# Layer 0 and 1 routing over 112 candidate sums, and more of the gathered rows' dots during routing than with the lots

## The reference

```
def peer(h, w_q, sub_keys, u_tab, v_tab):
    t = h.reshape(b * n, d)
    q = (t @ w_q).reshape(b * n, PEER_HEADS, 2, PEER_KEY_DIM)        # 8 heads
    s = jnp.einsum('thcd,hcnd->thcn', q, sub_keys)                   # 2 x 128 scores a head
    sv, si = lax.top_k(s, PEER_TOPK)                                 # 16 of each
    cand = (sv[:, :, 0, :, None] + sv[:, :, 1, None, :]).reshape(b * n, PEER_HEADS, 16 * 16)
    score, pos = lax.top_k(cand, PEER_TOPK)
    i1 = jnp.take_along_axis(si[:, :, 0], pos // PEER_TOPK, axis=-1)
    i2 = jnp.take_along_axis(si[:, :, 1], pos % PEER_TOPK, axis=-1)
    expert = i1 * PEER_KEYS + i2
    gate = softmax(score)
    ...
        act = gelu(einsum('td,thkd->thk', tb, jnp.take(u_tab, eb, axis=0)))
        return einsum('thk,thkd->td', gb * act, jnp.take(v_tab, eb, axis=0))
```

## Time and profile before

| | us |
|---|---|
| median of 3 runs | 3322.03 |
| lowest, highest run | 3318.63, 3327.59 |
| profiled execution | 3330.15 |
| its span | 3328.3 |
| TensorE busy in the span | 3179.4 |
| VectorE busy | 2511.7 |
| ScalarE busy | 1465.8 |
| GpSimd busy | 1061.4 |

### The profile page before, as it was taken

How to read it: one execution, slowest core, us unless ns; L and a number is a source line. 1 busy time by engine, 2 the same in 40 slices (tenths; PEclk the granted TensorE clock), 3 DMA queues, 4 the chain that set the end, 5 groups by cost and what they waited for, 6 DMA issues and landing times.

```text
span 3328.3 us, 52861 instructions
## 1 busy us (share of the span) xinstructions
PE 3179.4 (96%) x20142; PEld 2921.5 (88%) x20142; DVE 2511.7 (75%) x4061; ACT 1465.8 (44%) x1864; POOL 1061.4 (32%) x706
## 2 busy tenths in 40 slices
PE   7999889999999999999999999999988999999999
PEld 5998689856777899999999999997868898989998
DVE  6877568686764489988749999897665797757777
ACT  5434344322443333366643333334234567864443
POOL 0110000010000278877673334451000698721110
PEclk9999899999999999999999999999999999999999
DMA  8984157461012267799999999994203578999996
GB/s 320 332 307 170 51 190 247 157 227 64 1 39 102 98 233 272 264 326 383 363 399 390 381 378 411 410 410 169 89 1 121 182 242 294 388 367 335 352 342 232
DMA packets 305610, 835.27 MB, mean 251 GB/s; under 512 B 22432, under 2 KB 185504, under 8 KB 254368
## 3 DMA queue, kind: packets, MB, share of 16 engines
q1 hardware_dynamic: 180096, 534.82, 44.2%
q0 software_dynamic: 67968, 247.49, 19.3%
q10 hardware_dynamic: 57376, 50.72, 4.5%
HBM read 750.10 MB, written 82.84 MB: 250 GB/s over the span
## 4 chain that ended last, share of the span: by engine, by line
PE 73%; DVE 13%; DMA 5%; ACT 3%; issue 2%; POOL 2%; SPq 1%; ACTq 0%; DVEq 0%; POOLq 0%
PE ps L3369 16%; PE ps L862 7%; PE ps L3352 6%; PE ps L1688 5%; PE ps L2909 5%; PE ps L873 4%; PE ps L2310 3%; PE ps L2933 3%; PE ps L3354 3%; PE ps L319 3%; DMA gates<-arena 3%; PE ps L2911 3%; PE ps L1430 2%; PE ps L1412 2%; DVE arena L2968 2%
## 5 line engine op out<-in xcount | busy, mean ns | idle before, releaser
L2883 POOL TENSOR_TENSOR arena_split<-ring,arena_split 128x1024 fp32r<-128x1024 f32 x228 | 569.5, 2512 | 886.5 <-ACT arena_split L2801 883.7
L2933 PE MATMUL ps<-xT_split,arena_split 128*128 128x384 f32 x2048 | 535.1, 337 | 4.0 <-ACT xT L2831 3.2
L3369 PE MATMUL ps<-arena_split 128*128 128x384 f32 x3072 | 532.7, 334 | 1.0 <-DVE arena_split L3292 1.0
L3369 PEld LDWEIGHTS ps<-arena_split 128*128 128x128 f32 x3072 | 532.4, 188 | 1.3 <-issue 1.3
L286 DVE TENSOR_TENSOR arena_split<-ring,arena_split 128x2048 fp32r<-128x2048 f32 x128 | 292.9, 2291 | 245.8 <-ACT arena_split L280 244.9
L3263 ACT ACTIVATE arena_split<-ring 128x2048 fp32r<-128x2048 f32 x126 | 241.7, 1918 | 504.3 <-PE ps L3369 314.7
L280 ACT ACTIVATE arena_split<-ring 128x2048 fp32r<-128x2048 f32 x128 | 244.4, 1915 | 378.3 <-PE ps L862 133.3
L2933 PEld LDWEIGHTS ps<-xT_split,arena_split 128*128 128x128 f32 x2048 | 372.1, 188 | 5.3 <-issue 4.2
L3289 DVE TENSOR_TENSOR arena_split<-ring,arena_split 128x2048 fp32r<-128x2048 f32 x128 | 293.3, 2291 | 98.9 <-ACT arena_split L3263 92.8
L557 POOL DMA_DIRECT2D arena<-in_side_weights x152 | 82.8, 546 | 824.2 <-DVE arena L577 288.5
L2909 PE MATMUL ps<-hT_split,arena_split 128*128 128x448 f32 x1024 | 338.7, 379 | 6.7 <-POOL arena_split L2883 4.5
(11 more groups left out here) (353 smaller groups left out, 6377.1 us busy)
## 6 DMA issues: line engine op xcount, KB each, us to landing
ring<-in_weights SPq DMA_DIRECT2D x396, 1024.0 KB
arena<-in_side_weights POOLq DMA_DIRECT2D x152, 512.0 KB
gates<-arena SPq DMA_DIRECT2D x76, 512.0 KB
arena<-gates SPq DMA_DIRECT2D x32, 768.0 KB
arena<-activations SPq DMA_DIRECT2D x64, 384.0 KB
activations<-xT ACTq DMA_DIRECT2D x128, 112.0 KB
arena<-gates SPq DMA_DIRECT2D x32, 448.0 KB
arena<-activations SPq DMA_DIRECT2D x64, 224.0 KB
```

Source lines behind the costliest of these rows:

```text
L2883: pool.tensor_tensor(low, self.raw(f)[:, j, :], high.bitcast(F32), ALU.subtract)\
L2933: mm = pe.matmul(k.ps[:, j, 0:self.T], self.u[:, 2 * (f % 2) + j, a, t * P:(t + 1) * P], self.h[b][:, t, :], start=n == 0, stop=n == 3 * D ...
L3369: mm = pe.matmul(k.ps[:, t, self.from_token:self.from_token + self.T], self.v[:, f % 2, a, j * D + t * P:j * D + (t + 1) * P], self.weight ...
```

## The change

There are two parts.

The sums are formed only where they can be among the 16 largest, in two blocks: list places 0 to 3 of the first list with all 16 of the second (64 sums), and places 4 to 15 of the first with 0 to 3 of the second (48 sums). That makes 112 in place of 256, and `top` runs over rows of 112. A place found below 64 splits as before (by 16); one from 64 on splits by 4, and its first part is place / 4 - 12. This applies to both layers.

The dots of layer 0 are spread anew: 20 in place of 12 in each of tiles 1 to 3, so at each pause one or two, and one dot with each lot. That is 60, 48 and 20 in place of 36, 72 and 20. `pair_of` follows, and with it the places of the gathers in GpSimd's queue.

```diff
+PAUSES = 14
+BLOCKS = ((0, 4, 16, 0), (4, 16, 4, 64))
+CANDIDATES = 112
...
-        self.per_tile, self.pauses = 12, 0
+        self.per_tile, self.pauses = 20, 0
...
-            self.pair_of += [c] * 3
+            self.pair_of += [c] * LOTS_PER_PAIR[0]
...
         self.pauses += 1
-        if self.pauses % 7:
+        while self.taken < self.per_tile * self.pauses // PAUSES:
             self.dot(dve)
...
-        sums = self.sums.rearrange("p h (a b) -> p h a b", b=t)
-        chain(dve.tensor_tensor(sums, v[:, :, 0, :].unsqueeze(3).to_broadcast([P, h, t, t]),
-                                v[:, :, 1, :].unsqueeze(2).to_broadcast([P, h, t, t]), ALU.add))
+        for lo, hi, n, at in BLOCKS:
+            sums = self.sums[:, :, at:at + (hi - lo) * n].rearrange("p h (a b) -> p h a b", b=n)
+            ins = dve.tensor_tensor(sums, v[:, :, 0, lo:hi].unsqueeze(3).to_broadcast([P, h, hi - lo, n]),
+                                    v[:, :, 1, 0:n].unsqueeze(2).to_broadcast([P, h, hi - lo, n]), ALU.add)
+        chain(ins)
...
-        dve.tensor_scalar(self.ia.bitcast(U32), self.si.bitcast(U32), 4, None, ALU.logical_shift_right)
-        chain(dve.tensor_scalar(self.ib.bitcast(U32), self.si.bitcast(U32), 15, None, ALU.bitwise_and))
-        dve.tensor_copy(self.ha, self.ia.bitcast(U32))
-        chain(dve.tensor_copy(self.hb, self.ib.bitcast(U32)))
+        place, by16, by4, mask = (x.bitcast(U32) for x in (self.si, self.ia, self.ib, self.fa))
+        dve.tensor_scalar(by16, place, 4, None, ALU.logical_shift_right)
+        dve.tensor_scalar(by4, place, 2, None, ALU.logical_shift_right)
+        chain(dve.tensor_scalar(mask, place, 64, 12, ALU.is_lt, ALU.mult))
+        dve.scalar_tensor_tensor(self.ha, by4, -12.0, by16, ALU.add, ALU.max)
+        chain(dve.scalar_tensor_tensor(self.fb.bitcast(U32), mask, 3, place, ALU.bitwise_or, ALU.bitwise_and))
+        chain(dve.tensor_copy(self.hb, self.fb.bitcast(U32)))
...
-                for _ in range(1 + q):
-                    gather.dot(dve)
+                gather.dot(dve)
```

More of the change, by code:

```diff
@@ L2680, in __init__ @@
         next(at)
-        self.sums = k.room(next(at), PEER_HEADS, PEER_TOPK * PEER_TOPK)
+        self.sums = k.room(next(at), PEER_HEADS, CANDIDATES)
         self.sv, self.si, self.ia, self.ib, self.fa, self.fb = (k.room(next(at), PEER_HEADS, PEER_TOPK) for _ in range(6))
```

## The result

The changed kernel takes 3343.78 us, the median of 5 runs (3338.35 to 3349.19), against 3324.24 for five runs of the kernel before: a ratio of 1.0056, 95% interval 1.0043 to 1.0069. It is slower by 0.56%, and the forecast (3320.4, range 3307 to 3335) missed: its time lies above the range, on the side of rival B and past it. The profiled execution took 3344.82 us (span 3343.0), 14.7 more than that of before. That is less than the 19.5 between the medians, since the profiled run of before lay 6 us above its median.

A forecast was written before the change was run, and what follows sets the result against it. TensorE, busy 96% of the span, was taken as the bound. Layer 0's routing +10.9, lots -8.0, the stage's end -1.5 and layer 1 -3.0 summed to -1.6 us, so 3320.4 us, range 3307 to 3335.

The forecast's parts named there:

- rival B: Layer 0's routing: GpSimd and VectorE wait for each other in a ring; +9 to +20 us, about 3334; chance 0.18.
- VectorE's dots and the narrower rows: Layer 0's routing from 1213.8 us: 24 more dots, +29.3, less 3 tiles at 7.1 saved, +8.0 us.
- rival D: Lots: relief does not come, as block stores are late by SP's queue order; +8, so 3330; chance 0.10.
- The stop at pair 9: Layer 0's routing: a seventh gather waits for the second dot, so TensorE stops some 4 us.
- The wait at the turn: Where layer 0's routing ends: TensorE waits 3 to 8 us for VectorE, a sign of being right.
- one clock loss: Behind layer 0's turn: a stop of 4 us drops TensorE's granted clock, costing +1.4 us.
- the two terms: Relief in the lots, -8.0 us with bound -9.3, and at the stage's end, -1.5 with bound -3.2.
- the port term: Layer 0's routing: VectorE's waiting grows with GpSimd's share through added gathers; +1.5 us, bounds -11.2 and +10.
- These stops are not added to the sum: Layer 0's routing: TensorE's stops for GpSimd cost nothing extra while they total less than the slip.
- the sum's slip: Layer 0's routing: 8.0 + 1.5 + 1.4 = +10.9 us, from 0 to +22.
- Layer 1, -3.0 forecast: Layer 1's routing: 14.2 us less VectorE work shortens TensorE's waits; -3.0 us, from -2 to -7.
- The first wait goes whole: Layer 1's turn: TensorE's wait of 2.3 us there vanishes entirely.

The follow-up runs named there:

- s3: Changed kernel with 12 gathers and dots a tile, plus 24 further products needing no gather in tiles 1 to 3; 3332.28 us, 1.0020 of the kernel before.
- s1: Changed kernel with the old distribution of dots, so the 112 sums alone; 3323.26 us, 0.9996 of the kernel before.
- s7: Changed kernel with first gathers behind pair 6, not 8, and dots' expected pairs from 5, not 7; 3338.19 us, 1.0045 of the kernel before.
- s11: Changed kernel with GpSimd's subtractions halved in only pairs 30 to 32 of layer 0; 3338.69 us, 1.0038 of the kernel before.
- s5: Changed kernel with GpSimd's subtractions halved in pairs 9 to 32 of layer 0; 3331.68 us, 1.0022 of the kernel before.

## Why the prediction was wrong

**What held.** VectorE's dots and the narrower rows: +8.0 forecast, +7.6 measured in s3, and the same in the changed kernel. In the lots TensorE's 7.9 us of waits for ScalarE's copies went whole, and with them the copies' 19.6 us of waits for the stores of gate blocks, so rival D is out. The stop at pair 9: about 4 us forecast, 4.27 measured, and for the reason given, the seventh gather. The wait at the turn (3 to 8 forecast) was 5.9. The DMA share in the lots was set too low, 0.89 against 0.97, without harm.

**What agreed by luck.** From the turn to the values -8.1 was forecast (-9.5, and +1.4 for one clock loss) and -9.3 measured. The clock loss was 3.3, more than twice its term, and the relief some 12, where the bounds of the two terms, -9.3 and -3.2, make 12.5; the two misses cancel.

**The step that failed is the port term, "If waiting grows with that share it adds +1.5".** VectorE's standing grew by 7.9 us, near the upper bound of +10 that stood beside the term, and 2.9 us of waits for rows came on top, which the prediction named as what would break it. The share was the wrong measure. In s1, where GpSimd has no gather more than before, standing grew from 13.8 to about 22 us as well, while in s3 it stayed at 14.0, and in the three long cases in routing an instruction began within 0.5 us of the start of a pair of subtractions. So it depends on how the two sequences fall against each other, and a mean rate does not give it. The estimate also counted the two products alone. Their standing fell, from 11.2 to 9.1; that of the small L2985 and L2996, with pieces of 5.07 and 4.41 us, which it left out, went from 2.6 to 12.5.

**A term was missing: from routing's end to the turn, +6.6.** The sum counted VectorE's work up to the last dot and took the last steps as unchanged. The earlier trace rows showed L3035 at 0.56 us, with GpSimd idle around it. Now two steps stand 7.9 us for subtractions and one waits 1.65 for the exponential, less the 3.1 of standing that was there before. The prediction said that GpSimd "hardly catches up", and did not carry this on to the last steps.

**"These stops are not added to the sum" held by luck.** "Some 4 us" and "1 to 5 us at two or three later pairs" make 6 to 19 us, and 15.8 were measured, so their size was right but for the clock that goes with them, 5.2 us. But the sum's slip was 10.9 us, and stops of 21 are more than that: had VectorE been as little late as forecast and the stops been these, TensorE's own arrival would have set the turn more than 20 us late. The stops stayed hidden only because VectorE's delay was larger too. Two delays of one size lie side by side there, and whoever repairs one meets the other: s7 took 7.4 us of stops away and was left with a wait of 8.2, s11 took 4.7 us of the wait away and was left with the stops.

**Layer 1, -3.0 forecast, -1.2 measured.** "The first wait goes whole" is the step that failed there. By the shortest instance of each instruction some 12 us of work went, but standing grew from 29 to 35, so VectorE's routing got 6.0 shorter. Of this the turn sees 1.2, since VectorE then stands in the casts and waits for the exponential, which comes at almost the same place as before (152.6 us behind the start of routing, 153.3 before), and behind it the last steps take their 15.6 us, 16.0 before. The earlier trace rows showed for whom TensorE waits, but not for whom VectorE does.

**Together:** -1.6 forecast. To it come 15.4 in layer 0's routing (port +6.4, rows +2.9, last steps +6.6, work -0.4), -1.2 between the turn and the values and +1.8 in layer 1, so +14.4. The profiles differ by 14.7; the remaining +0.3 is 3.3 before the first dot less 3.1 in stretches that the change does not touch, both of a size that comes and goes between executions. Rival B had the mechanism, engines that wait for each other in a ring, and its "+9 to +20" holds the 14.4 and the medians' 19.5, though its time of 3334 lies in the low half. Its condition, two or more further products that meet a pair of subtractions whole, did not come: one product did (7.11 us), as before (7.45). Small instructions and the last steps stood for pairs instead. Its 0.18 was too little. What spoke for B were the row of 7.45 us and the full queue; against it I set that four of six products had stood for little, which says where the meetings had fallen so far, and nothing about where they would fall once everything moved.

**Not settled.** How much of the 19.5 us is the stops and how much VectorE's delay can't be split, since they lie beside each other, and no run shortened only GpSimd's queue or only VectorE's standing. Why the standing falls as it does (14.0 in s3, 22 in s1) was not derived, only read, and so was why some instructions get in between two subtractions and others stand for both. The dip of the clock at the first transposes stood in all profiles with the 112 sums or the 20 dots but s5's, and in neither of the two profiles without; whether the change brings it about is open, and it is worth 1.5 us. None of the versions beats the kernel before beyond its interval.

## What to carry to other kernels

Where the rows show that two engines stand for each other's instructions, work added to both is paid twice: by its own time, and by where it pushes the instructions of one against those of the other. So ask of every step behind the added work who had been idle beside it, and price that idle time. A cheap control tells whether the other engine's instructions bind: halve them in both kernels, and see in which the time moves. It shortens that engine's queue too, so it doesn't say by which way they bind. And work taken off a path wins only up to the next releaser, which is best looked up in the waits of the engine that is sped up, before the sum is made.

## What was not expected of the hardware

Two subtractions of GpSimd, issued back to back, can hold up a VectorE instruction for nearly their whole 4.8 us (7.11, 5.07 and 4.41 us for instructions that else take 2.29, 0.27 and 0.22). A cast with a single input is held just so, the 5.07. It isn't always so: L3009 at 1349.25 got in between two of them and took 3.32 us in place of 1.22, and in layer 1 the casts at 2763.67 and 2765.96, of 2.37 and 2.42 us, each ended with one subtraction of an unbroken row of five. In the other direction a gather's issue takes up to 2.98 us in place of 0.95 beside VectorE's fp16 product. And stops of 4.3 to 6.7 us each bring the granted clock of the 18 to 20 us around them to 0.87 to 0.91, some 5 us of work over three stops, a third of what the stops themselves took.
